# Decoder layer with a hierarchical MoE: normalized rows kept without the affine part, the first expert pair's rows from one-hot products, gate rows summed on GpSimd

## The reference, cut to what matters

```python
h = x * (1.0 + scale1) + shift1                 # ada = silu(c) @ w_ada + b_ada, six rows of 1024
proj = h @ w_in                                 # q k v (8 heads of 64) and three conv inputs
attn = stick_breaking_attention(q, k, v)        # strictly causal, 512 tokens
conv = cb * causal_depthwise_conv(cc * cx, conv_w)
mix  = concat([attn, conv]) @ w_out
x    = layer_norm(2**0.25 * x + gate1 * mix, ln1_g, ln1_b)
h2   = x * (1.0 + scale2) + shift2
# group_logits = h2 @ w_rg + b_rg, top 1 of 4; exp_logits = h2 @ w_re + b_re, top 2 of that group's 8
y    = sum over 32 experts: combine[:, e] * (silu(h2 @ w_gate[e]) * (h2 @ w_up[e])) @ w_down[e]
x    = layer_norm(2**0.25 * x + gate2 * y, ln2_g, ln2_b)
```

## Time and profile before

| what | us |
|---|---|
| runs: median (lowest to highest of 3) | 551.41 (549.99 to 551.89) |
| profiled execution: span, first to last instruction | 550.1 |
| PE, DVE, ACT, POOL busy | 509.8, 285.4, 105.5, 101.6 |
| span to the first expert's `gates` | 303.6 |
| experts, `gates` of the first to `gates` of the last | 303.6 to 519.4 |

### The profile page before, as it was taken

The page is one execution under the profiler, slowest core; times in us unless marked ns, Lnnn a source line. Parts: engine busy times, 40 slices in busy tenths (PEclk is TensorE's granted clock), DMA queues, the critical chain, the costliest instruction groups (busy, mean ns, idle before and its releaser), DMA issues.

```text
span 550.1 us, 6473 instructions
## 1 busy us (share of the span) xinstructions
PE 509.8 (93%) x2516; PEld 274.5 (50%) x2516; DVE 285.4 (52%) x520; ACT 105.5 (19%) x173; POOL 101.6 (18%) x111
## 2 busy tenths in 40 slices
PE   3999999999999999999996999999998799898983
PEld 2445468744444444444583555555554355444531
DVE  4664999763937393263889732232222122213388
ACT  1000211233223231200232311111111111121030
POOL 2000000061306040030452111111211011210015
PEclk9999999999999999999997999999999899989998
DMA  8999679954640244269998999999999999999763
GB/s 254 358 361 352 207 237 309 309 212 153 227 155 1 77 146 174 75 245 418 413 391 310 388 405 420 414 416 417 414 417 416 416 415 416 416 416 418 312 251 153
DMA packets 71280, 169.22 MB, mean 308 GB/s; under 512 B 7902, under 2 KB 45842, under 8 KB 63056
## 3 DMA queue, kind: packets, MB, share of 16 engines
q1 hardware_dynamic: 64304, 152.22, 73.2%
q10 hardware_dynamic: 2480, 8.44, 4.0%
q0 software_dynamic: 4464, 8.12, 3.9%
HBM read 159.60 MB, written 17.30 MB: 322 GB/s over the span
## 4 chain that ended last, share of the span: by engine, by line
PE 61%; DVE 14%; DMA 11%; SPq 9%; issue 3%; ACT 1%; POOL 0%; DVEq 0%; POOLq 0%; ACTq 0%
PE ps L1622 17%; PE ps L1492 11%; PE ps L1538 10%; PE ps L1631 9%; DVE acc_rows L935 5%; SPq L414 4%; DMA w_gu<-in_w_up_dram 4%; PE ps L1612 3%; PE ps L1462 3%; DMA ada_stage<-in_w_ada_dram 3%; DMA w_stage<-in_w_in_dram 2%; PE ps L1481 2%; DMA y_tok<-y_dram 2%; PE ps L1526 2%; DMA y_dram<-ysb,slot_row 1%
## 5 line engine op out<-in xcount | busy, mean ns | idle before, releaser
L1622 PE MATMUL ps<-w_gu,xT 128*64 128x256 f32 x1024 | 119.3, 386 | 3.4 <-issue 1.6
L1622 PEld LDWEIGHTS ps<-w_gu,xT 128*64 128x64 f32 x1024 | 72.0, 138 | 40.5 <-issue 3.4
L1492 PE MATMUL ps<-hT,w_stage 128*128 128x512 f32 x192 | 84.8, 595 | 0.0
L1256 DVE TENSOR_TENSOR ysb<-ps,rows_gate 64x512 f32<-64x512 f32 x64 | 44.1, 689 | 61.8 <-PE ps L1631 61.3
L1631 PE MATMUL ps<-w_dn,hidT 128*64 128x512 f32 x256 | 62.9, 612 | 7.8 <-issue 6.1
L935 DVE SCALAR_TENSOR_TENSOR acc_rows<-ada_stage,csil,acc_rows 128x256 f32<-128x256 f32 x112 | 55.2, 493 | 4.0
L1247 DVE TENSOR_TENSOR hid<-ps,silu_sb 128x128 f32<-128x128 f32 x32 | 9.3, 292 | 91.9 <-ACT silu_sb L846 91.9
L1492 PEld LDWEIGHTS ps<-hT,w_stage 128*128 128x128 f32 x192 | 35.5, 190 | 41.0 <-issue 41.0
L1538 PE MATMUL ps<-wo,mixT 128*128 128x512 f32 (+1 forms) x144 | 55.6, 545 | 0.0
L1403 PE MATMUL ps<-hT,w_first 128*128 128x512 f32 x96 | 45.5, 621 | 0.9 <-DVE hT L961 0.9
L627 POOL DMA_INDIRECT y_dram<-ysb,slot_row x15 | 15.1, 1009 | 151.8 <-DVE ysb L1256 151.8
(11 more groups left out here) (213 smaller groups left out, 499.2 us busy)
## 6 DMA issues: line engine op xcount, KB each, us to landing
w_gu<-in_w_gate_dram SPq DMA_DIRECT2D x32, 1024.0 KB, 20.3
w_gu<-in_w_up_dram SPq DMA_DIRECT2D x32, 1024.0 KB, 23.3
w_dn<-in_w_down_dram SPq DMA_DIRECT2D x32, 1024.0 KB, 24.3
ada_stage<-in_w_ada_dram SPq DMA_DIRECT2D x16, 1024.0 KB, 7.8
w_stage<-in_w_in_dram SPq DMA_DIRECT2D x9, 1024.0 KB, 10.1
ada_in<-in_w_ada_dram SPq DMA_DIRECT2D x12, 512.0 KB, 9.5
y_dram<-zeros ACTq DMA_DIRECT2D x4, 1024.0 KB, 5.8
wo<-in_w_out_dram SPq DMA_DIRECT2D x2, 2048.0 KB, 13.3
```

The source lines that it names most:

```text
L1256: ins = w.tensor_tensor(to[e * HD:(e + 1) * HD, b * 512:(b + 1) * 512], ps[b * HD:(b + 1) * HD, down_bank(y), :], gate2r[b * HD:(b + 1) * ...
L1492: ins = t.matmul(ps[:, 6], st[:, k, (f % 2) * P:(f % 2 + 1) * P], hT[:, k], start=k == 0, stop=k == KC - 1)
L1622: ins = t.matmul(ps[a * SLOTS:(a + 1) * SLOTS, GATE_BANK[e], 0:2 * P], rows_in[:, k, e * SLOTS:(e + 1) * SLOTS], weights[:, :, k, a * P:(a ...
```

## The change

- **Rows.** `xs` now keeps (x - mean) / deviation, written by one DVE pass (`h2_done`), and this is what is stored to `h2_dram`, transposed and gathered. The affine part is applied after each transpose, where channels are on the partitions: a scale `a2c` and a shift `b2c` per channel. For that PE sums shift2 and scale2 by columns (`sum_mod2`, 16 products with one column of ones, after the first conv projection), and ACT applies it as an activation per 128 x 128 block. In the expert loop ACT takes blocks 0 to 3 of each pair and DVE blocks 4 to 7 (`turn_out`).
- **Gate rows.** gate1 and gate2 are no longer spread by PE. GpSimd sums them over the partitions with `partition_all_reduce`, 128 x 512 at a time: two after head 1's masks, one after head 5's, one after the last. All products with ones (L1526) and the three idle products of L1606 go.
- **Places.** `hT` lies where `acc_rows` lay. Expert loads 0 and 1 wait for the twelfth conv projection and the last ada chunk; down of expert 5 is loaded with the fourth expert's; gate of 5 and down of 4 after the last piece, and the second half of slot 7 after all of x1.
- **Output projection.** The fourth k block is multiplied last, so that the last head pair's copy is not waited for; `mix` multiplies in place in PSUM. PE runs route(1) and transpose(2) ahead of the last piece, and then waits for the last tile's rows.
- **First pair.** No gather. DVE makes one-hot rows `hot_x` for experts 0 and 16 (three tiles, then the last), PE multiplies them with `xs` (`first_rows`), ACT applies the affine part block by block. The table of slots moves into the first `gates`, ahead of its fifth block.
- **x1.** Tiles 0 and 1 are made by DVE in `mix`'s loop into `x1_rows`; tiles 3 and 2 by DVE as before, but after the first pair's products, which read `xs`.

The core of the diff:

```diff
-            sp.wait_ge(row_done, 6)
+            sp.wait_ge(conv_done, len(CONV_OUT))
             sp.wait_ge(ada_done, len(COLS) + NADACH - ADA1)
@@ pool
+            def sum_row(r):
+                row, half = divmod(r, 2)
+                pool.wait_ge(ada_done, len(COLS) + 12 * row + 2 * half + 2)
+                g.partition_all_reduce((gate1r, gate2r)[row][:, half * 512:(half + 1) * 512], acc_gates[r][:], P,
+                                       bass.bass_isa.ReduceOp.add).then_inc(row_summed, 1)
...
+                if h == 1:
+                    sum_row(0)
+                    sum_row(1)
+                if h == 5:
+                    sum_row(2)
+            sum_row(3)
@@ vector
+                w.tensor_scalar(xs[:, i], xs[:, i], mv[:, i, 0:1], rstd[:, i:i + 1], ALU.subtract, ALU.mult
+                                ).then_inc(h2_done, 1)
...
-            dve.wait_ge(normed, TC)
-            dve.wait_ge(scaled, 2)
-            for i in X1_BY_DVE:
+            dve.wait_ge(xe_done, 1)
+            for n in range(2):
+                dve.wait_ge(st_h2[n], 32)
+            for i in X1_HELD:
                 w.tensor_tensor(xs[:, i], xs[:, i], g1r[:], ALU.mult).then_inc(x1_last, 1)
@@ tensor
-            pe.wait_ge(hot_done, 1)
-            for c in range(8):
...
-            for n in range(3):
-                t.matmul(ps[:, ROW_BANK[6]], ones[:], gate2r[:, 0:512], start=True, stop=True)
...
+                def first_turned(k):
+                    if k < KC - 1:
+                        pe.wait_ge(xe_half_ev, k + 1)
+                    else:
+                        pe.wait_ge(xe_ev, 1)
+                    if k == KC // 2:
+                        slot_table()
```

More of the change, by code:

```diff
@@ L1259, in y_out, with turn_out @@
                 ins.then_inc(y_ev, 1)
+            def turn_out(j):
+                dve.wait_ge(xe_done, j + 1)
+                for k in range(KC // 2, KC):
+                    ins = w.tensor_scalar(xT[rows_buffer(j)][:, k], turned_rows(j, k), a2c[:, k:k + 1], b2c[:, k:k + 1],
+                                          ALU.mult, ALU.add)
+                ins.then_inc(xe_ev, 1)
             def pair(j):
@@ L1614, in expert_rows, with gate_up @@
+            def expert_rows(j, rows, sem_done):
+                for k in range(KC):
+                    ins = t.transpose(turned_rows(j, k), by_channel(rows)[:, k], ident[:])
                 ins.then_inc(sem_done, 1)
-            def gate_up(e, rows_in, weights, sem_done, second_half=None):
+            def gate_up(e, rows_in, weights, sem_done, ahead=None):
                 for k in range(KC):
-                    if second_half is not None and k == KC // 2:
-                        pe.wait_ge(second_half, 1)
+                    if ahead is not None:
+                        ahead(k)
```

452 lines of the change are left out of this document (234 added, 218 removed).

## The result

The changed kernel takes 574.19 us (median of 4 runs, 573.32 to 574.69) against 551.65 us (549.99 to 552.19) of the kernel before on the same chip: ratio 1.0415, 95% interval 1.0396 to 1.0434. It is slower, as forecast, but by 22.5 us where 4.9 were forecast, and it lies outside the range. The profiled execution has a span of 571.1 us against 550.1, so 21.0 us are to be found.

The account below looks back on a forecast made before the run. The weight stream was taken to set the end: second expert issue +5.9, less 2.7 in flight, plus 1.7 restart, gives +4.9 on the 550.1 span, 555.0; with 1.3 to the median, 556.3 us. Range 551.5 to 563.5.

Parts of the forecast that it names:

- What bounds: End of the kernel: the weight stream sets the end, not PE; what counts is when the stream becomes continuous.
- -2.7 + 1.7: Stream at the load of expert 9: 2.7 us already in flight offset its delay, 1.7 us for restarting from nothing.
- `sum_mod2`: Attention stage: 32 fp32 records on PE take 3.4 us, 0.5 of it in idle time, +2.7 us on the path.
- Spread rows and order: Output projection: spread rows go, -5.5 us; route(1) and transpose(2) ahead of the last piece, +2.6 us.
- Sums on GpSimd: Attention stage: the first two sums take 8 us each, hidden in 10.8 us of cover each, cost 0.
- The rival of long sums: Attention stage: sums over 10.8 us shift everything behind by twice the excess; 16 us each give 566.7 us; chance 0.18.
- Last tile: From the last projection piece to `mb`: the end of `mb` stays to within 0.5 us, cost 0.
- First pair: First expert pair: one-hot products take 1.71 us per 16 records; first `gates` done 4.1 us earlier, table at 301.4.
- Tile 0 fits ahead of the counts: First pair: tile 0's one-hot products run while PE waits for `mb`, with counts done at 293.9.
- DVE's row behind the table: Table to first `hidden`: 10.2 us of DVE work starts 5.0 later; PE idles 8.8 us, clock loss 2.0.
- The range: Whole kernel: 551.5 to 563.5 us holds 0.8, leaving out the faster case and the far part of long sums.

## Why the prediction was wrong, point by point

- **What bounds.** Right. The load of expert 9 moved by 22.2 us and the span by 21.0; what lies behind it changed by -1.2 where the sum had -2.7 + 1.7 = -1.0. PE still had 10.3 us of waits in 97 at the end (86.75 busy from 440 to 537). The first expert load went out at 230.70, not at 224, since the attention stage was later; as said, this is worth nothing, for the stream ran dry twice behind it. That -1.2 meets -1.0 may be partly luck: the two terms were not measured apart.
- **`sum_mod2`.** The step that failed first: "the router's 16 small ones take 1.71, so 32 records take 3.4". It took 7.5, and with the clock behind it the attention stage ended 8.97 later, not 2.7. The row was taken for a product of its size, without a look at how its operand is read: the router's is contiguous, this one has a step of eight. The run that reads blocks gives the price back. The clock was not in this sum; the prediction looked for its fall only where PE is idle. (3.4 less 0.5 is also 2.9 and not 2.7, a slip without effect.)
- **Spread rows and order.** Right: -2.49 against -5.5 + 2.6 = -2.9.
- **Sums on GpSimd.** Right in effect, since hidden, and wrong in size: 3.2 us for one where 8 were taken. Ahead of the first stand 5.7 us with nothing in the profile, near the 6 us which the Trainium skill gives for a first call (GPSIMD Engine Reference, section 2.1). The estimate of 62 us by a linear reading of its section 3.2, which is for another instruction, does not hold for this one. The rival of long sums fell. In the changed kernel the first two lie in DVE's idle time (below), which the prediction did not look at; the run of the kernel before with more sums shows what that is worth.

```profile
140.91 0.69 DVE L1001 TENSOR_TENSOR u_conv<-ps,cc_sb 128x512 f32<-128x512 f32 x1 [20.12 <-PE ps L1518]
```

- **Last tile.** 0 was forecast for the steps from the last piece to `mb`, +1.4 came. The logits ended 1.1 later behind the last piece, as they ran at half clock (3.60 instead of 1.98), and `mb` 0.3 later behind the logits, as `hot_x` (0.56 us) stands between DVE's steps.
- **First pair.** The step that failed most: 1.71 for 16 records, with an upper bound of double that "at half clock". At full clock they took 3.9, above this bound, for the step of eight again. And "Tile 0 fits ahead of the counts" failed: its rows `hot_x` are made between the steps of the last `choose`, so it ran from 300.1 to 304.1 and the counts waited 2.7 us for it. From `mb` to the table it was 16.9 us, with 7.9 forecast.
- **DVE's row behind the table.** Right: 10.18 us, and PE idle for 8.76 where 8.8 was said, with the clock at 0.50 behind it. From `hidden` to the second issue it took 5.72, where 6.3 was said.
- **The range.** Its upper end came from the sums on GpSimd. The one-hot products, 64 records, had their bounds from one row; the measured price of the 48 records behind the counts, 11.7 us where 5.1 were taken, adds 6.6 us to the sum, the late tile 0 another 2.7, and the clock in the attention stage adds 2.2. The double price of the products was named as a bound but did not go into the range; the other two were in no bound.

What is open: why the clock held behind 3.6 to 3.7 us of one-column products in two places and fell behind them in two others; why transposes with a step of eight do not pay for it; what the strided read costs at steps other than eight and one, which was not tried. With the one-hot part undone 11.0 us of the loss remain, 8.4 of them by the end of attention (227.08 instead of 218.72).

## What to carry to other kernels

Price a product by how its stationary operand is read, and not by its shape alone: an fp32 product with a step of eight elements cost twice as much here, a transpose with that step did not. What stands ahead of a table that another engine waits for costs its whole length, since that engine's own row starts only behind the table; look for the products that can go behind it, and then for the next wait, which can take the gain back. And work moved to an idle GpSimd was free here only where DVE was idle beside it.

## What the runs showed of the hardware

- `partition_all_reduce` of 128 x 512 fp32 on GpSimd took 3.2 us, with 5.7 us ahead of the first in which nothing is shown.
- A product with 128 x 128 fp32 weights: 0.113 to 0.122 us per record contiguous, 0.24 with a step of eight elements, at full clock, whether it moves 1 column or 128; at half clock 0.24 and 0.26. Transposes with the same step took 0.14 a record (1.13 us for eight), contiguous ones 0.13 (1.29 for ten).
- DVE's pass over 128 x 256 fp32 (`scalar_tensor_tensor`) took 674 ns with its output and one input at a step of 128 elements, 485 without.
- Beside two sums on GpSimd, DVE's steps of 0.48 and 0.75 us took 1.75 and 2.66, and the two sums 7.75 instead of 6.49.
- The granted clock fell with PE busy without a gap, in 7.5 us of products of one column (mean 0.52 in 120 to 125). At the router it fell with PE idle for 0.26 us, in products of 40 columns, in the run where no product of 512 stood between them (mean 0.70 in 285 to 290).
